# A sample's output mix as full 4-byte products before the weights are split, and the prompt's mix halves moved forward

## The reference, cut to what matters

```python
h = modulate(norm(x), c)                  # adaLN conditioning, one row set for the prompt, one for the sample
u, q, k, v = split(h @ w_in)              # 512 columns for pooling, 3 x 512 for attention (8 heads of 64)
pooled = trailing_mean(u) - u
mixed = einsum('bngc,gcd->bngd', pooled, w_pool) * pool_scale
att = stick_breaking(q, k, v)             # sigmoid, suffix products, then weights @ v
y = concat(mixed, att) @ w_out            # 1024 x 1024, "the mix"
x1 = layer_norm(ALPHA * x + gate * y)
hn2 = modulate(norm(x1), c)
out = layer_norm(ALPHA * x1 + gate2 * moe(hn2))   # 16 experts in 4 groups, 2 of them for each row
```

## Time and profile before

| | |
|---|---|
| median of 3 runs | 804.96 us |
| profiled execution, its own time | 804.16 us |
| its span in the trace | 802.4 us |
| granted TensorE clock, mean | 0.979 |
| TensorE busy | 767.7 us, 96% |
| TensorE weight loads busy | 606.4 us, 76% |
| VectorE busy | 562.9 us, 70% |
| ScalarE busy | 374.6 us, 47% |
| GpSimd busy | 309.9 us, 39% |
| mix products of wo_hi with mixin (L1279) | 256 instructions, 82.9 us busy |

### The profile page before, as it was taken

One profiled execution on the slowest core, in us unless ns is written; L12 is line 12 of the kernel. 1 busy time (PEld: TensorE's weight loads), 2 busy tenths in 40 slices (PEclk: granted clock), 3 DMA queues, 4 the chain that ended last, 5 costly groups with the idle time before them and its releaser, 6 DMA issues. The chain is left out here.

```text
span 802.4 us, 13449 instructions
## 1 busy us (share of the span) xinstructions
PE 767.7 (96%) x4808; PEld 606.4 (76%) x4809; DVE 562.9 (70%) x621; ACT 374.6 (47%) x706; POOL 309.9 (39%) x261
## 2 busy tenths in 40 slices
PE   7999999999989899999999997799999999999995
PEld 4889999999975566767767786488888888888641
DVE  5759957762125995876787867998656999574178
ACT  4571212212246983554464528544444444544254
POOL 2100799990010300100000110367565899564156
PEclk9999999999999999999999996899999999999997
DMA  8947644715049701320202249967779998889695
GB/s 320 388 153 257 210 158 133 228 53 185 1 149 327 236 2 53 106 80 27 80 27 79 80 158 333 338 249 262 259 269 361 415 376 270 294 315 364 238 372 200
DMA packets 78442, 168.59 MB, mean 210 GB/s; under 512 B 6974, under 2 KB 32126, under 8 KB 76219
## 3 DMA queue, kind: packets, MB, share of 16 engines
q1 hardware_dynamic: 69154, 134.36, 47.9%
q0 software_dynamic: 8048, 29.36, 9.9%
q10 hardware_dynamic: 1192, 4.21, 1.5%
HBM read 132.57 MB, written 33.12 MB: 207 GB/s over the span
## 5 line engine op out<-in xcount | busy, mean ns | idle before, releaser
L2501 PE MATMUL psum<-we_hi,x_parts 128*128 x384 | 136.5, 402 | 0.8 <-ACT x_parts L2257 0.8
L2045 DVE TENSOR_TENSOR we_lo<-we_raw,we_hi 128x2048 fp32r<-128x2048 f32 x48 | 118.0, 2461 | 1.5
L490 PE MATMUL psum<-hn_hi,w_hi 128*128 128x364 f32 (+1 forms) x380 | 91.2, 332 | 1.3 <-DVE hn_lo L716 1.3
L490 PE MATMUL psum<-hn_lo,w_hi 128*128 128x364 f32 (+1 forms) x380 | 90.3, 329 | 0.0
L490 PE MATMUL psum<-hn_hi,w_lo 128*128 128x364 f32 (+1 forms) x380 | 90.0, 328 | 0.0
L2044 DVE CAST we_hi<-we_raw 128x2048 fp32r<-128x2048 f32 x44 | 59.6, 1355 | 39.5 <-DMA we_raw<-in_w_up_dram 25.6
L1279 PE MATMUL psum<-wo_hi,mixin 128*128 128x512 f32 (+1 forms) x256 | 82.9, 395 | 1.6 <-DVE logits L1646 1.1
L2501 PEld LDWEIGHTS psum<-we_hi,x_parts 128*128 128x128 f32 x384 | 72.1, 188 | 15.3 <-issue 1.1
L2501 PE MATMUL psum<-we_lo,x_parts 128*128 x192 | 75.4, 393 | 0.0
L793 DVE SCALAR_TENSOR_TENSOR proj<-early,cT,proj 128x2048 f32<-128x2048 f32 x28 | 72.1, 2616 | 1.5 <-DMA early<-in_w_mod_dram 1.3
L490 PEld LDWEIGHTS psum<-hn_hi,w_hi 128*128 128x128 f32 x380 | 66.6, 189 | 4.7 <-issue 2.3
(11 more groups left out here) (376 smaller groups left out, 1569.2 us busy)
## 6 DMA issues: line engine op xcount, KB each, us to landing
we_raw<-in_w_up_dram SPq DMA_DIRECT2D x32, 1024.0 KB, 8.4
early<-in_w_mod_dram SPq DMA_DIRECT2D x16, 1024.0 KB, 5.4
we_raw<-in_w_down_dram SPq DMA_DIRECT2D x16, 1024.0 KB, 7.0
w_raw<-in_w_in_dram SPq DMA_DIRECT2D x16, 512.0 KB, 6.2
we_raw<-ff_d SPq DMA_DIRECT2D x12, 512.0 KB, 7.2
proj<-in_x_prompt_dram SPq DMA_DIRECT2D x4, 1024.0 KB, 8.0
sc_room<-in_w_mod_dram SPq DMA_DIRECT2D x4, 1024.0 KB, 11.0
wo_raw<-in_w_out_dram SPq DMA_DIRECT2D x2, 2048.0 KB, 9.4
```

The lines of the kernel that those rows point to most:

```text
L490: mm = pe.matmul(psum[:, 2 * c + slot, 0:n], w[:, slot, k, :], hn[:, k, t0:t0 + n], start=(k == 0 and w is w_hi and hn is hn_hi), stop=(k ...
L2045: dve.tensor_tensor(we_lo[:, a:b], raw, we_hi[:, a:b].bitcast(F32), ALU.subtract).then_inc(ready, 1)
L2501: mm = pe.matmul(psum[:, bank, :], x[:, s, k, :], w[:, bass.ds(at + k * 2 * DE, 2 * DE)], start=(k == 0 and x is x_hi and w is we_hi), sto ...
```

## The change

The sample's mix leaves the table's steps M0:0 and M1:0 and becomes four steps MS:0 to MS:3 beside units 12 to 15. Each takes two of the eight row blocks. It multiplies the unsplit rows (proj) with the unsplit weights (wo_raw) as 4-byte values. The left column half goes to partitions 0 to 63 of bank 7 and the right one to 64 to 127. The split of the sample's rows (Ph:0, Pl:0) goes. The low halves of the weights, which overwrite wo_raw, now wait for that mix, and the first of them moves from unit 15 to unit 16. The pooling maps are made in another order, the four pieces of the sample first. The sample's gate products move from units 28 and 29 to units 16 and 17, and all steps of the prompt's tiles move forward by two to four units. The list of TensorE's steps after the last unit stays as it was.

```diff
 PE_BESIDE = {
     3: "PM:0", 4: "PM:1", 5: "PM:2", 6: "PM:3", 7: "PM:4", 8: "PM:5", 9: "PM:6", 10: "PM:7", 11: "PM:8",
-    20: "PM:9", 23: "PM:10", 25: "PM:11", 28: "M0:0", 29: "M1:0", 31: "M0:1", 33: "M1:1", 34: "T0:0", 35: "M0:2", 36: "T1:0",
-    37: "M1:2", 38: "T2:0", 39: "R:0", 40: "M0:3", 41: "T0:1", 42: "M1:3", 43: "T1:1", 44: "M0:4", 45: "T2:1",
-    46: "M1:4", 47: "R:1", 48: "M0:5", 49: "T0:2", 50: "T1:2", 51: "M1:5", 52: "T2:2", 53: "M0:6", 54: "R:2",
-    55: "M1:6", 56: "T0:3", 57: "M0:7",
+    12: "MS:0", 13: "MS:1", 14: "MS:2", 15: "MS:3", 20: "PM:9", 23: "PM:10", 25: "PM:11",
+    28: "M0:1", 30: "M1:1", 31: "T0:0", 32: "M0:2", 33: "T1:0", 34: "M1:2", 35: "T2:0", 36: "M0:3", 37: "R:0", 38: "M1:3",
+    39: "T0:1", 40: "M0:4", 41: "T1:1", 42: "M1:4", 43: "T2:1", 44: "M0:5", 45: "R:1", 46: "M1:5",
+    47: "T0:2", 49: "T1:2", 50: "M0:6", 51: "T2:2", 52: "M1:6", 53: "R:2", 55: "M0:7", 56: "T0:3",
...
 ACT_BESIDE = {
-    26: "Ph:0", 29: "Ph:1", 30: "Q1:0", 31: "Q2:0", 33: "Ph:2", 34: "Q1:1 H0:0", 35: "Q2:1", 36: "H1:0",
...
+    26: "Ph:1", 28: "Q1:0", 29: "Q2:0", 30: "Ph:2", 31: "Q1:1 H0:0", 32: "Q2:1", 33: "H1:0",
...
 DVE_BESIDE = {
-    1: "DV:0", 7: "DV:1", 8: "DV:2", 9: "DV:3", 10: "DV:4", 11: "DV:5", 12: "DV:6", 13: "DV:7", 14: "DV:8", 15: "wl:0", 16: "wl:1", 18: "wl:2", 19: "wl:3", 20: "wl:4", 21: "wl:5", 23: "wl:6", 25: "wl:7", 26: "Pl:0", 28: "C0:0",
-    29: "C1:0 R:0 Pl:1", 30: "E1:0 G1:0", 31: "B1:0 C0:1 E2:0 G2:0", 32: "B2:0", 33: "C1:1 R:1 Pl:2", 34: "E1:1 G1:1",
...
-    55: "G2:4 B2:4 C1:6 R:6 Pl:7", 56: "E1:6 G1:6 B1:6 G2:5 E2:6 B2:5 G2:6 C0:7",
+    1: "DV:0", 7: "DV:1", 8: "DV:2", 9: "DV:3", 10: "DV:4", 11: "DV:5", 12: "DV:6", 13: "DV:7", 14: "DV:8", 16: "wl:0 C0:0", 17: "C1:0 wl:1",
+    18: "wl:2", 19: "wl:3", 20: "wl:4", 21: "wl:5", 23: "wl:6", 25: "wl:7", 26: "Pl:1", 27: "R:0", 28: "E1:0 G1:0 C0:1",
+    29: "B1:0 E2:0 G2:0 B2:0", 30: "C1:1 R:1 Pl:2", 31: "E1:1 G1:1", 32: "B1:1 C0:2 E2:1", 34: "G2:1 B2:1 C1:2 R:2 Pl:3",
...
+    48: "B1:5 E2:5", 50: "G2:3 B2:3 C0:6", 52: "C1:6 R:6 Pl:7", 53: "E1:6 L:2", 54: "G1:6 B1:6 E2:6", 55: "C0:7",
+    56: "G2:4 B2:4 G2:5", 57: "B2:5 G2:6",
...
-        POOL_PIECES = ((0, 512), (512, 512), (SEQ, DEC))
+        PIECES = [(g, SEQ, DEC) for g in range(4)] + [(g, t0, 512) for g in range(4) for t0 in (0, 512)]
+        RAW_PARTS = 4
...
+            def mix_sample(m):
+
+                if m == 0:
+                    pe.wait_ge(att_copied, PAIRS)
+                    pe.wait_ge(pool_copied, 4)
+                    for half in range(2):
+                        pe.wait_ge(wo_loaded[half], 16)
+                    take("MS", 0, (mix_copied, 2))
+                for k in range(m * KC // RAW_PARTS, (m + 1) * KC // RAW_PARTS):
+                    for half in range(2):
+                        mm = pe.matmul(psum[DEC * half:DEC * half + DEC, 7, :], proj[:, k, SEQ:NT],
+                                       wo_raw[:, k, 512 * half:512 * half + 512], start=(k == 0), stop=(k == KC - 1))
+                if m == RAW_PARTS - 1:
+                    mm.then_inc(mix_done, 2)
...
             def mix(n, half):
-                pe.wait_ge(mix_lo_ready, n + 1)
+                pe.wait_ge(mix_lo_ready, n)
...
             def low_wo(n):
                 dve.wait_ge(wo_hi_ready, n + 1)
+                dve.wait_ge(mix_done, 2)
...
             def copy_mix(n, half):
-                gate = g1[0:r, 512 * half:512 * half + 512]
-                dve.tensor_tensor(tile_of(n)[:, 4 * half:4 * half + 4, :], by_chunk(bank(f"M{half}", n)[0:r, :]), by_chunk(gate),
+                at = DEC * half if n == 0 else 0
+                gate = g1[at:at + r, 512 * half:512 * half + 512]
+                dve.tensor_tensor(tile_of(n)[:, 4 * half:4 * half + 4, :], by_chunk(bank(f"M{half}", n)[at:at + r, :]), by_chunk(gate),
                                   ALU.mult).then_inc(mix_copied, 1)
```

More of the change, by code:

```diff
@@ L1211, in pool_map @@
             def pool_map(n):
-                g, (t0, w) = n // 3, POOL_PIECES[n % 3]
+                g, t0, w = PIECES[n]
                 out = take("PM", n, (pool_copied, n + 1))
@@ L1353, in _ @@
                         pool_map(n)
+                    elif step == "MS":
+                        mix_sample(n)
                     elif step in ("M0", "M1"):
@@ L1443, in high_mix @@
                 act.wait_ge(pool_copied, 12)
-                if 0 < n < TILES - 1:
+                if n < TILES - 1:
                     act.wait_ge(mix_done, 2 * n)
@@ L1571, in low_mix @@
                 r, j = rows(ORDER[n]), ORDER[n]
-                dve.wait_ge(mix_hi_ready, n + 1)
+                dve.wait_ge(mix_hi_ready, n)
                 dve.tensor_tensor(mix_room(n)[:, 1, :, 0:r], proj[:, 0:KC, j * P:j * P + r], mix_room(n)[:, 0, :, 0:r].bitcast(F32),
```

## The result

The changed kernel is slower: 819.96 us median of 5 runs (815.18 to 820.57) against 805.84 of 5 runs before (803.80 to 807.60) on the same chip. The ratio over all these runs is 1.0157, with a 95% interval of 1.0128 to 1.0185 (ratios here are taken over all runs and can differ a little from that of the two medians). Five more rounds on another chip gave 817.60 against 806.40, 1.0135 (1.0107 to 1.0163). The forecast was 803.5. The profiled execution has a span of 818.2 us, at a mean granted clock of 0.960; before it was 802.4.

What follows compares the result with a forecast made beforehand. TensorE was taken to set the length from 298 to 481 us. Removed products 11.3 us less 8.5 delay, less a 2.2 stall, plus 0.9 idle time gone: 1.5 won, 804.96 to 803.5 us; range 798.7 to 807.3.

Steps and rivals of the forecast that it cites:

- The sample's part: Mix in units 12 to 15: four steps of 1.89 us, 7.5 in all; unit 16's scores 6.4 us late, unit 28 8.5.
- the bounds: For the sample's four new TensorE steps together: 7.5 us with column halves fully overlapping, 14.5 us without overlap; 7.5 was taken.
- the 0.2 ahead of unit 12: Units 7 to 11: the new order of pooling pieces adds 0.2 us of delay on TensorE.
- the 7 to 9.5 that the prediction allowed itself: At unit 28, the first prompt half: the forecast is wrong if it is less than 7 or more than 9.5 us late.
- The stall before M0:2: TensorE stands 2.2 us: VectorE needs 16.4 us to tile 1's low half, with G2 waiting for x1's store; TensorE needs 14.2.
- from tile 2 on the same sum leaves TensorE the later one by over 1 us: Prompt halves from tile 2 on: VectorE's low half is ready over 1 us before TensorE needs it, with no store wait.
- the 3.2 of the forecast: TensorE's idle time among the prompt's halves: a 2.2 us stall before M0:2, and 1.0 of the present 1.88 us coming back.
- The third rival: More operand waits: 2.2 us stalls at two more places (M1:3 behind R:0, M1:5 behind R:1), 807.9 us; chance 0.10.
- Nothing after 481 us waits for a thing of its own: After the last mix, through first gather and expert stage: a microsecond won or lost before it is one at the end.

Runs made afterwards that it cites:

- without the store's wait: The copies first kernel with the sample's x1 moved to the room of the turned rows, so G2 needn't wait for its store: 806.92 us against 806.40, 1.0011.
- copies first: Changed kernel with Q2:5 and E2:5 one unit later, and ScalarE's copies H ahead of squares Q1 in five units: 808.50 us against 806.40, 1.0027.
- the long hold: Kernel before the change with six unread ScalarE copies (1.06 us each) ahead of the copy of unit 41's attention result: 814.75 us against 807.09, 1.0092.
- the sample's part alone: Changed kernel with the sample's early mix in units 12 to 15, but the prompt's steps at before's order and place: 805.23 us against 805.88, 0.9992.
- five unread products: The kernel without the store's wait, with five instead of four unread TensorE products ahead of the first gather's landing: 805.14 us against 807.09, 0.9978.

## Why the prediction was wrong

**The sample's part: right.** The step was forecast at 1.89 us and takes 1.77, at the end of the bounds that was taken. Unit 16's scores are 7.8 us late against 6.4 forecast. 2.3 of it are there before the first MS step (unit 12's scores start at 261.78, not 259.44), and these move between executions: with the same tables up to there, unit 12's scores start at 258.42 without the store's wait, 259.47 with the copies first and 263.15 in the second profile of the changed kernel. Two things ahead of them move. One is the landing of a transfer that unit 8's scan stands behind on VectorE, as the prediction saw. The other is the clock: 241.3 to 248.1 at the lower level here, none with the copies first, 258.1 to 261.6 in the second profile of the changed kernel, there behind a gap of 3.46 us that this landing made:

```profile
256.37 0.69 DVE L1548 TENSOR_TENSOR dv<-dv,hi_room 128x512 f32<-128x512 f32 x1 [6.53 <-DMA dv<-hi_room]
257.77 0.37 PE L1179 MATMUL psum<-plus,ring_bits 128*128 128x128 f32 x2 [3.46 <-DVE ring L1577]
```

How the 2.3 us divide between the two, the profiles don't say. From unit 12's scores on, these four agree: 12.6 us to unit 16's scores (7.15 before) and 47.1 us to the first prompt half (308.87 less 261.78), where the kernel before takes 39.7 to the sample half (299.10 less 259.44). That is a delay of 5.5 and 7.4 us, against 6.2 and 8.3 forecast behind the 0.2 ahead of unit 12. With the 2.3 the first prompt half was 9.8 us late, just outside the 7 to 9.5 that the prediction allowed itself.

**The stall before M0:2: place and size about right, the cause in part not.** 2.2 us were forecast behind the store's wait; 0.99 + 1.77 came. Taking away the store's wait gave back 1.0 us of the interval, though by a way not forecast, C1:1 and bank 7. The copy standing behind a square, which the prediction didn't look at, had 0.9. The 0.86 left is the low half's.

**The step that failed: "from tile 2 on the same sum leaves TensorE the later one by over 1 us".** The sum was made for VectorE's way to the next low half, and for that it holds: no later mix half waits for mixin. But the mix halves are not the only work that waits. ScalarE's queue also holds the squares, and the attention copies behind them; in the new order Q2:5 comes ahead of a copy that TensorE needs, and waits itself for B1:5. That is the 3.52 us gap, and moving one square by one unit removed it (1.0135 or 1.0157 to 1.0078). The prediction should have followed each moved step on ScalarE as it did on VectorE: what is queued behind it, and who waits for that. With the smaller ones (1.6, 0.6) TensorE idles 9.5 us after 309, not the 3.2 of the forecast (2.2 and 1.0).

**The term that was missing: the clock.** All microseconds were priced at the 2.4 GHz level that the kernel before has from 298 to 481 us. Gaps of this size have a second price: 1.4 to 2.0 us behind the one of 3.5, 1.7 behind the one of 4.5, and 1.5 to 2.2 behind the pair at M0:2 (11.9 and 12.6 against 10.4). Two short gaps (1.24 and 0.82) had none. The third rival, two more stalls of 2.2 us and 807.9, named the right mechanism, operand waits of the new order, but at M1:3 and M1:5 TensorE stood for only 1.16 and 0.48 us, the large waits were elsewhere, and it had no price for the clock; its chance was 0.10.

**"Nothing after 481 us waits for a thing of its own" and so the rest is unchanged: wrong by some 4 us in the profile.** From the last mix's end to the end it is 325.6 us (492.65 to 818.2), before 321.3 (481.07 to 802.4). The first product of the first gathered rows starts 31.7 us behind the last mix (524.37), 30.5 before (511.59), and the long stretch at the lower clock that covers this passage lasts from 497.3 to 521.2, before from 488.3 to 508.8. At 528 and 777 us the clock is at the lower level for 3.4 us each, so up to 1.7 us of loss each, with TensorE full all the while; before has no such stretch at these places. The kernel with the long hold has both too. The kernel with the copies first has a stretch at 763.7 to 767.1, and 325.0 us after the last mix, though nothing in its attention fell: so these stretches are not simply the echo of the gaps, and what calls them stays open.

**The sum of the profile.** The last mix ends at 492.65, forecast 479.6 (481.07 less 1.5): 13.1 us late. The first prompt half was late by 1.3 (308.87 against 307.6), the idle time 6.3 over (9.5 against 3.2), and the clock behind the two gaps cost 4.2 (2.2 and 2.0); 1.3 are not assigned. With 4.3 after the mix this is 17.4, against 818.2 - (802.4 - 1.5) = 17.3 us between the profile and its forecast.

**By the ratios,** each step of the mending stands against before: changed +1.35%, Q2:5 later +0.78%, copies first +0.27%, no store wait +0.11%. In microseconds 10.9, 6.3, 2.2, 0.9. That these edits remove the loss is shown. That the mended order and the sample's part alone win nothing by more than these runs can tell is shown as well, by 1.0011 and 0.9992.

Why they win nothing can be followed in the profiles, one of each kernel. 11.3 us of mix products go and 7.1 (4 x 1.77) come, 4.2 less. From unit 12's scores to the first prompt half 3.9 of these are still there (11.3 less 7.4, the same in the four profiles above), so what lies between, VectorE's backlog of units 16 to 23 and idle time that is filled, takes 0.3 on balance. From unit 12's scores to the last mix's end it is 219.3 us without the store's wait, 220.3 with the copies first and 219.5 with the sample's part alone, against 221.6 before: 1.3 to 2.3 us are won there. Behind the last mix, 324.2, 325.0 and 322.4 us stand against 321.3, so 1.1 to 3.7 are lost. The experiment with five unread products has 322.2 there and the shortest span (801.1 against 802.4). Why that part gets longer stays open; no experiment here takes it apart.

## What to carry to other kernels

When steps of a hand-written order are moved, walk the queue of every engine, the idle ones too: a short copy that TensorE needs is as late as whatever waits in front of it, and a square that waits for another engine's mean is best put behind such copies. Price a stall on TensorE twice, as its own length and as the clock behind it: here a gap of 2 us in two pieces cost 2.3, one of 4.5 us cost 6.2. And do part and rest of a change apart before blaming its main part: here the new arithmetic was free, and one table entry of the reordering made nearly half of the loss. Compare marks ahead of the changed place and behind it too: in the profile without the store's wait, 2.9 of the 3.3 us won up to the last mix were lost behind it.

## What the runs showed of the hardware

- 4-byte products with 64 stationary columns overlap fully when they go to different halves of the partitions, whatever their order: four of 512 columns take 1.77 us with the halves alternating or not, 3.4 us in one half.
- The granted clock can fall inside a gap of TensorE or shortly behind it. With the gap of 4.50 us (to 400.41) it falls at 397.7, and full work from 401 to 404.5 runs at the 1.2 GHz level. The gap of 3.52 us at unit 46 is followed by a fall at 429.0 in one profile of the changed kernel, inside the gap, and in the other at 432.2, when TensorE has worked again since 431.55:

```profile
431.55 0.94 PE L1269 MATMUL psum<-early,dv 128*64 128x128 f32 x12 [3.52 <-ACT proj L1447]
```

- The lower level after the same gap can last 6.8 us (429.0 to 435.8) or 3.4 us (432.2 to 435.6); the interval around it was 22.7 and 22.1 us.
- The place of some stretches at the lower level changes from one execution of the same kernel to the next: 241.3 to 248.1 in one profile of the changed kernel, 258.1 to 261.6 in the other.
